# A trunk of four layers on one NeuronCore: GpSimd makes one weight tile's low half behind each running-mean mixer, and the first block's means and its add into h move forward

## The chip, the cores and the metric

The kernel runs on one core of one Trainium2 chip. The metric is the device time in microseconds, the median of several executions. Lower is better.

## What is computed

The input x has 512 tokens of 1024 channels; 16 meta tokens stand ahead of it, so the trunk works on 528 tokens. Four layers follow, each a mixer and a SwiGLU feed-forward network (FFN), and a final norm. Layers 0 and 3 have the running-mean mixer, layer 1 differential attention, layer 2 a conformer convolution. Cut to what matters here:

```python
def pool_mixer(h, w, b, scale):                 # layers 0 and 3
    for g, win in enumerate((2, 4, 8, 16)):
        hg = h[..., g * 256:(g + 1) * 256]
        groups.append(trailing_mean(hg, win) - hg)
    pooled = jnp.stack(groups, axis=2)
    mixed = jnp.einsum('blgc,gcd->blgd', pooled, w).reshape(B_, L, D_MODEL)
    return (mixed + b) * scale

for i in range(DEPTH):
    y = rmsnorm(h, norm_mix_g[i])
    h = h + mixer(y)
    h = h + (silu(n @ w_gate) * (n @ w_up)) @ w_down      # n = rmsnorm(h, norm_ffn_g[i])
```

All is float32.

## The kernel before

**Split operands.** TensorE multiplies rounded operands (fp32r). Each operand is cut into a high half, which is the value rounded (ScalarE, `ACT.Copy` into an fp32r tile), and a low half, the value less the high one (VectorE). A product is then three matmuls: high by high, low by high, high by low. For a weight tile, ScalarE's `split_hi` makes `w_hi` from `w_raw` and VectorE's `split_lo` (L2258, the instruction is L2264) makes `w_lo`. For the activations ScalarE makes `y_hi` (L1762) and VectorE `y_lo` (L2267, instruction L2270).

**Weight tiles.** The weights come as a long row of tiles of up to 128x1024 through four slots of `w_raw`, `w_hi` and `w_lo`. SyncE loads a tile into a slot when `lo_ready`, a semaphore that counts the low halves made so far, has passed the slot's last user. `hi_ready` counts the high halves. TensorE waits for `lo_ready` before it uses a tile. The mixer's own four tiles are `tile0` to `tile0 + 3`; tiles `tile0 + 4` and `tile0 + 5` are the first gate and up tiles of the FFN behind it.

**Layout.** Channels lie on partitions: `h` has 8 blocks (`blk(m.h, d)`) of 128 channels by 528 tokens. The norm's factor of a token is applied later, where tokens are on partitions or to the product, so `y_hi` and `y_lo` of block d need only h of block d and the gain column.

**The mixer** first multiplies the weights with tokens on partitions, in five tiles of tokens (`rows_times_weights`, L1004; 128, 128, 128, 127 and 32 rows). ScalarE and VectorE bring the products, scaled by the token's norm factor, from PSUM into `z_hi` (L1823) and `z_lo` (L2394, five instructions, each counted by `z_ready`). Then `windows(d)` multiplies block d of z by a band matrix, which takes the running means less the value itself (L1043, L1044, L1045 and L1052), tile after tile into two PSUM banks; with the last tile's matmul it counts `pooled`. VectorE's `add_windows(d)` (L2366) adds the block, times the scale, into h and counts `h_ready`. The bias comes into h ahead of that: by ScalarE in layer 0, by GpSimd (L933, eight adds) in layer 3.

**Behind the mixer** stands the head of the FFN (`head_by_blocks`, L1082). TensorE's stream there: six unread rows (matmuls whose result nobody reads, L1090), the means of blocks 0 and 1 without their last tile of 32 tokens, the last tile of both, eight unread rows, the means of block 2, four unread rows, the wait for `lo_ready` of the two FFN tiles, and then, block by block, the FFN's first products (`chunk`, L946) with the means of block k + 3 behind block k. In the means of block 0, `z_of` waits for four z tiles before the first and for the fifth before the last; block 1 has no such wait. `windows(d)` for d of 2 and more waits for h of block d - 2, whose banks it takes over.

VectorE's queue in the same place: the five `z_lo`, `split_lo` of tile 4, `add_windows(0)`, `split_lo` of tile 5, `y_lo` of block 0, then `add_windows(1)`, and further on alternately. ScalarE's: the five `z_hi`, `split_hi` of tiles 4 and 5, then `y_hi` and the square of each block (L1833). GpSimd adds up the squares (`sum_squares`, L799: a memset of `sumsq` at L808, then a loop of eight adds at L819, each behind a semaphore), which TensorE sums over channels at the end of the head (L960).

All orders are written out by hand; each engine runs its own queue in order, and the engines meet at semaphores.

Of the kernel before, what the change touches and what calls it, by code (L numbers as in the profile page):

```python
# [27 lines left out]
F32 = mybir.dt.float32  # L28
F32R = mybir.dt.float32r
I32 = mybir.dt.int32  # L30
ALU = mybir.AluOpType
# [27 lines left out]
TILES = 5  # L59
# [13 lines left out]
SLOTS = 4  # L73
# [481 lines left out]
def trunk(nc, a, out):  # L555
    cols, first = plan()
    tiles = len(cols)
    ctx = ExitStack()
    with ctx:
        m = Memory(nc, ctx)  # L560
# [201 lines left out]
        def _(pool):  # L762
# [36 lines left out]
            def sum_squares(r, hn):  # L799


                wait(pool, s.token_sums, r)
                wait(pool, s.rstd_sums, spreads(r))
                if r not in SUMS_OF_SQUARES:
                    pool.wait_ge(s.h_ready, NB * hn + 1)
                elif r in (R_FFN1, R_POOL3):
                    pool.wait_ge(s.square_ready, squares_before(r) + 1)
                pool.memset(m.sumsq[:, :], 0.0)  # L808
                pool.drain()
                with pool.Fori(0, NB) as d:  # L810
                    if r in SUMS_OF_SQUARES:
                        pool.wait_ge(s.square_ready, d + (squares_before(r) + 1))
                        square = blk({R_FFN1: m.o_square, R_FFN2: m.cv_square}.get(r, m.x_square), d)
                    else:
                        pool.wait_ge(s.h_ready, d + (NB * hn + 1))
                        pool.tensor_tensor(m.square[:, :], blk(m.h, d), blk(m.h, d), ALU.mult)
                        pool.drain()
                        square = m.square[:, :]
                    pool.tensor_tensor(m.sumsq[:, :], m.sumsq[:, :], square, ALU.add).then_inc(s.sumsq_ready, 1)  # L819
                    pool.drain()  # L820


            pool.wait_ge(s.table_in, 16)
            pool.memset(m.rel[:, REL_N:], 0.0)
            for i0, n, b in bucket_runs():
                last = pool.tensor_copy(m.rel[:, i0:i0 + n], m.table[:, b:b + 1].to_broadcast([HEADS, n]))
            pool.drain().then_inc(s.rel_ready, 1)
            sum_squares(R_FFN0, H_POOL0)
            sum_squares(R_ATTN, H_FFN0)

# [100 lines left out]
            for d in range(NB):  # L931
                pool.wait_ge(s.y_ready, NB * Y_POOL3 + d + 1)
                pool.tensor_tensor(blk(m.h, d), blk(m.h, d), m.pool_bs[:, 1, d:d + 1].to_broadcast([P, TOK]), ALU.add)\  # L933
                    .then_inc(s.h_biased, 1)

            sum_squares(R_FFN3, H_POOL3)


        @block.tensor
        def _(pe):  # L940
# [134 lines left out]
            def pair_layer(name, n, e0, r, yn, hn, t0, half, conv=False, pooled=None):  # L1075
# [6 lines left out]
                def head_by_blocks():  # L1082

                    if pooled is None:
                        pe.wait_ge(s.h_ready, NB * hn + 4)
                    else:
                        def unread_rows(n):

                            for _ in range(n):
                                pe.matmul(ps[:, 2, 0:HALF], m.z_hi[:, 0, 0:P], m.z_hi[:, 0, 0:HALF], start=True, stop=True)  # L1090

                        pe.wait_ge(s.z_ready, TILES * pooled + 2)
                        unread_rows(6)
                        for d in range(2):
                            windows(d, pooled, hn, range(TILES - 1))
                        for d in range(2):
                            windows(d, pooled, hn, (TILES - 1,))
                        unread_rows(8)
                        windows(2, pooled, hn)
                        unread_rows(4)  # L1100
                    pe.wait_ge(s.lo_ready, tile0 + 2)
                    for k in range(NB):
                        pe.wait_ge(s.y_ready, NB * yn + k + 1)
                        for c in range(2):
                            if r == R_FFN1 and k == 0 and c == 1:
                                pe.wait_ge(s.h_ready, NB * hn + 7)
                            mm = chunk(2 * c, half, (tile0 + c) % SLOTS, k * P, operand(m.y_hi, k, t0, half),
                                       operand(m.y_lo, k, t0, half), k == 0, k == NB - 1)
                            if k == NB - 1:
                                mm.then_inc(s.tile_used, 1)  # L1110
                        if pooled is not None and k + 3 < NB:
                            windows(k + 3, pooled, hn)
                    sum_tokens(r)
# [1143 lines left out]
        def _(dve):  # L2257
# [99 lines left out]
            def pool_layer(name, which, r, yn, hn, row):  # L2357
# [32 lines left out]
                for i in range(TILES):  # L2390
                    base, n = 2 * (i % 4), TILE_ROWS[i]
                    dve.wait_ge(s.z_hi_ready, TILES * which + i + 1)
                    two = [t[0:n, i, :].rearrange("p (b n) -> p b n", b=2) for t in (m.z_lo, m.z_hi)]
                    dve.scalar_tensor_tensor(out=two[0], in0=ps[0:n, base:base + 2, :], scalar=m.tok_r[0:n, i:i + 1],  # L2394
                                             in1=two[1].bitcast(F32), op0=ALU.mult, op1=ALU.subtract)\
                       .then_inc(s.z_ready, 1)
                split_lo(tile0 + 4, 0, 0, cols[tile0 + 4])
                add_windows(0)
                split_lo(tile0 + 5, 0, 0, cols[tile0 + 5])
                y_lo(0, yn, row, 0, TOK)  # L2400
                for d in range(1, NB):
                    add_windows(d)
# [684 lines left out]
```

## Time and profile before

| | |
|---|---|
| median of 3 executions | 2008.43 us (2007.77 to 2008.64) |
| profiled execution, its own time | 2008.29 us |
| its span, first to last instruction | 2006.5 us |
| mean granted TensorE clock | 0.999 |
| TensorE matmul busy | 1989.3 us (99%) |
| TensorE weight load busy | 1934.6 us (96%) |
| VectorE busy | 1570.3 us (78%) |
| ScalarE busy | 915.4 us (46%) |
| GpSimd busy | 203.1 us (10%) |

The span is the time between the first and the last instruction of one execution; the execution's own time is 1.79 us longer. The first mixer's means begin at about 33 us of the span, the second's at about 1633 us. In the rows below the engines are PE (TensorE matmul), PEld (its weight loads), DVE (VectorE), ACT (ScalarE), POOL (GpSimd); an instruction reads `out<-in partitions x elements`, and a bracket at a row's end is the idle time before it and what released it.

### The profile page before, as it was taken

The numbers are of one execution on the slowest core, as the hardware profiler recorded it, in microseconds if no ns is written. First come the engines' busy times: TensorE is split into PE (matmuls) and PEld (weight loads), VectorE is DVE, ScalarE is ACT, GpSimd is POOL, SyncE is SP. The second block draws the span as 40 slices with busy tenths as digits, with TensorE's granted clock in tenths as the row PEclk, the third lists the DMA queues.
The fourth block names the chain that finished last, engine by engine and source line by source line (L and its number), as shares of the span: only waits on it lengthen the run. The fifth ranks groups of instructions, "written<-read, shape, count | busy, mean of one in ns | idle before, by whom it ended". The sixth has DMA issues, their size and how long they took to land.

```text
span 2006.5 us, 40536 instructions
## 1 busy us (share of the span) xinstructions
PE 1989.3 (99%) x16016; PEld 1934.6 (96%) x16016; DVE 1570.3 (78%) x2221; ACT 915.4 (46%) x1472; POOL 203.1 (10%) x317
## 2 busy tenths in 40 slices
PE   9999999999999999999999999999999999999998
PEld 8999999999998999999999999999999998999997
DVE  6797778767877788877869886697788768977794
ACT  7443334346666443433458755343343354433342
POOL 5000000331111200000051102000000140000000
PEclk9999999999999999999999999999999999999999
DMA  5423243332211224333336531233342423333332
GB/s 169 139 85 105 84 125 85 90 123 64 62 51 58 85 85 127 93 87 92 111 101 148 126 90 56 87 97 89 105 125 67 125 75 97 106 92 100 89 106 95
DMA packets 304529, 195.24 MB, mean 97 GB/s; under 512 B 7354, under 2 KB 297147, under 8 KB 304148
## 3 DMA queue, kind: packets, MB, share of 16 engines
q1 hardware_dynamic: 298972, 175.08, 30.5%
q0 software_dynamic: 4240, 14.09, 3.3%
q10 hardware_dynamic: 1192, 4.34, 0.6%
q8 instruction: 86, 1.41, 0.3%
q14 instruction: 39, 0.32, 0.1%
HBM read 179.45 MB, written 6.44 MB: 93 GB/s over the span
## 4 chain that ended last, share of the span: by engine, by line
PE 87%; DVE 6%; issue 2%; ACT 2%; DVEq 2%; DMA 1%; POOLq 0%; SPq 0%; POOL 0%; ACTq 0%
PE ps L946 43%; PE ps L1230 32%; PE ps L1069 2%; PE ps L1341 2%; PE ps L1004 1%; PE ps L1052 1%; PE ps L1413 1%; DVE w_lo L2264 1%; DVE w_lo L2503 1%; PE ps L1454 1%; DVEq L2539 1%; DVEq L2508 1%; DVE y_lo L2503 0%; DMA w_raw<-in_ffn_w_down 0%; DMA x_rows<-in_x 0%
## 5 line engine op out<-in xcount | busy, mean ns | idle before, releaser
L1230 PE MATMUL ps<-t_lo,y_hi 128*128 128x264 f32 (+1 forms) x1008 | 285.7, 283 | 0.0
L1230 PE MATMUL ps<-t_lo,w_hi 128*128 128x264 f32 (+1 forms) x1008 | 285.7, 283 | 0.0
L1230 PE MATMUL ps<-t_hi,w_lo 128*128 128x264 f32 (+1 forms) x1008 | 285.4, 283 | 0.0
L1230 PE MATMUL ps<-t_hi,y_lo 128*128 128x264 f32 (+1 forms) x1008 | 285.3, 283 | 0.0
L1230 PE MATMUL ps<-t_hi,w_hi 128*128 128x264 f32 (+1 forms) x1008 | 285.1, 283 | 0.1
L1230 PE MATMUL ps<-t_hi,y_hi 128*128 128x264 f32 (+1 forms) x1008 | 284.8, 283 | 0.0
L1881 ACT ACTIVATE w_hi<-w_raw 128x1024 fp32r<-128x1024 f32 (+1 forms) x108 | 127.8, 1201 | 329.4 <-PE ps L946 193.2
L946 PE MATMUL ps<-hid_hi,w_hi 128*128 128x264 f32 (+1 forms) x1184 | 265.4, 296 | 0.6 <-DVE hid_lo L2559 0.5
L946 PE MATMUL ps<-hid_lo,w_hi 128*128 128x264 f32 (+1 forms) x1184 | 264.6, 296 | 0.0
L946 PE MATMUL ps<-hid_hi,w_lo 128*128 128x264 f32 (+1 forms) x1184 | 264.2, 296 | 0.0
L946 PE MATMUL ps<-y_hi,w_hi 128*128 128x264 f32 (+1 forms) x1088 | 241.1, 298 | 1.8 <-POOLq L914 0.8
L946 PE MATMUL ps<-y_lo,w_hi 128*128 128x264 f32 (+1 forms) x1088 | 233.5, 291 | 0.0
L946 PE MATMUL ps<-y_hi,w_lo 128*128 128x264 f32 (+1 forms) x1088 | 233.4, 291 | 0.0
L1881 ACT ACTIVATE y_hi<-w_raw 128x1024 fp32r<-128x1024 f32 (+1 forms) x108 | 125.8, 1197 | 166.6 <-DVE w_raw L2513 133.9
L946 PEld LDWEIGHTS ps<-hid_hi,w_hi 128*128 128x128 f32 x1184 | 187.2, 188 | 7.2 <-DVE hid_lo L2559 1.6
L946 PEld LDWEIGHTS ps<-hid_lo,w_hi 128*128 128x128 f32 x1184 | 187.6, 188 | 5.5
L946 PEld LDWEIGHTS ps<-hid_hi,w_lo 128*128 128x128 f32 x1184 | 187.4, 188 | 5.6
L1230 PEld LDWEIGHTS ps<-t_hi,w_hi 128*128 128x128 f32 x1008 | 189.8, 188 | 0.6 <-DVE h L2599 0.5
L1230 PEld LDWEIGHTS ps<-t_hi,y_hi 128*128 128x128 f32 x1008 | 189.8, 188 | 0.0
L1230 PEld LDWEIGHTS ps<-t_lo,w_hi 128*128 128x128 f32 x1008 | 189.5, 188 | 0.1
L1230 PEld LDWEIGHTS ps<-t_hi,w_lo 128*128 128x128 f32 x1008 | 189.5, 188 | 0.0
L1230 PEld LDWEIGHTS ps<-t_hi,y_lo 128*128 128x128 f32 x1008 | 189.5, 188 | 0.0
(362 smaller groups left out, 4364.3 us busy)
## 6 DMA issues: line engine op xcount, KB each, us to landing
w_raw<-in_ffn_w_gate SPq DMA_DIRECT2D x88, 512.0 KB, 5.1
w_raw<-in_ffn_w_up SPq DMA_DIRECT2D x88, 512.0 KB, 4.8
w_raw<-in_ffn_w_down SPq DMA_DIRECT2D x70, 512.0 KB, 4.3
w_raw<-in_ffn_w_down SPq DMA_DIRECT2D x24, 384.0 KB, 4.3
w_raw<-in_attn_w_qkv SPq DMA_DIRECT2D x16, 512.0 KB, 3.8
w_raw<-in_conv_w_in SPq DMA_DIRECT2D x16, 512.0 KB, 4.1
w_lo<-w_raw POOLq DMA_DIRECT2D x16, 512.0 KB, 5.0
w_raw<-in_attn_w_qkv SPq DMA_DIRECT2D x16, 256.0 KB, 2.9
```

The costliest lines, as they stand in the source:

```text
L946: mm = pe.matmul(ps[:, bank + hf, 0:half], w[:, slot, col:col + P], x(hf), start=begin and w is m.w_hi and n == 0, stop=end and w is m.w_lo)
L1004: mm = pe.matmul(out, y[:, at:at + rows], w[:, (t0 + g) % SLOTS, k * 256:(k + 1) * 256], start=k == 0 and n == 0, stop=k == 1 and n == 2)
L1052: mm = pe.matmul(out[:, c0:c1], z, m.bands[0:TILE_ROWS[i], g, at:at + c1 - c0], start=i == 2 and n == 0, stop=i in (1, 4) and n == 1)
L1069: mm = pe.matmul(ps[:, 4 * par + 2 + r, 0:cols_n], w[rows, par, :, :].rearrange("p t c -> p (t c)")[:, pairs_of_taps], u[rows, par, (j - r ...
L1230: mm = pe.matmul(ps[:, bank, 0:hw], w[:, at:at + P], b[:, t, k, 0:hw], start=k == 0 and n == 0, stop=k == 3 and n == 2)
L1341: mm = pe.matmul(bank, x, w, start=False, stop=k == LAST_F - 1 and n == 2)
L1413: mm = pe.matmul(ps[:, (4, proj_banks(par, 1))[part] + c, col:col + k1 - k0], q[rows, 0, q0:q0 + P], k[rows, 1, k0:k1], start=n == 0, stop ...
L1454: mm = pe.matmul(ps[:, 4, i * P:QT * P], v, w, start=False, stop=i == QT - 1 and x == 2)
L1881: act.activation(hi[:, sub * SUB:(sub + n_sub) * SUB], src, ACT.Copy).then_inc(s.op_hi, 1)
L2264: dve.tensor_tensor(m.w_lo[:, slot, 0:n], m.w_raw[:, slot, 0:n], m.w_hi[:, slot, 0:n].bitcast(F32), ALU.subtract).then_inc(s.lo_ready, 1)
L2503: dve.tensor_tensor(lo[:, at], raw_of(kind, c0, c1), hi[:, at].bitcast(F32), ALU.subtract)\
L2508: dve.drain()
```

## The change

Three engines' orders change, behind both mixers.

- TensorE: block 0's last tile of means stands ahead of block 1, and block 1 is done whole behind it. The unread rows ahead of block 2 are six instead of eight.
- VectorE: `add_windows(0)` comes first behind the five `z_lo`, then `split_lo` of tile 4. `split_lo` of tile 5 is gone, so that `y_lo` of block 0 follows directly.
- GpSimd: a new function, `second_tile`, waits for tile 5's high half, makes its low half, drains, waits until `lo_ready` has counted all tiles before it, drains again and counts `lo_ready`. It is called ahead of the sum of squares for the FFN's norm; in layer 3 that is behind the eight bias adds.

```diff
--- before.py
+++ after.py
@@ -820,11 +820,21 @@
                     pool.drain()
 
 
+            def second_tile(t):
+
+                pool.wait_ge(s.hi_ready, t + 1)
+                pool.tensor_tensor(m.w_lo[:, t % SLOTS, :], m.w_raw[:, t % SLOTS, :], m.w_hi[:, t % SLOTS, :].bitcast(F32),
+                                   ALU.subtract)
+                pool.drain()
+                pool.wait_ge(s.lo_ready, t)
+                pool.drain().then_inc(s.lo_ready, 1)
+
             pool.wait_ge(s.table_in, 16)
             pool.memset(m.rel[:, REL_N:], 0.0)
             for i0, n, b in bucket_runs():
                 last = pool.tensor_copy(m.rel[:, i0:i0 + n], m.table[:, b:b + 1].to_broadcast([HEADS, n]))
             pool.drain().then_inc(s.rel_ready, 1)
+            second_tile(first["pool0"] + 5)
             sum_squares(R_FFN0, H_POOL0)
             sum_squares(R_ATTN, H_FFN0)
 
@@ -933,6 +943,7 @@
                 pool.tensor_tensor(blk(m.h, d), blk(m.h, d), m.pool_bs[:, 1, d:d + 1].to_broadcast([P, TOK]), ALU.add)\
                     .then_inc(s.h_biased, 1)
 
+            second_tile(first["pool3"] + 5)
             sum_squares(R_FFN3, H_POOL3)
 
 
@@ -1091,11 +1102,10 @@
 
                         pe.wait_ge(s.z_ready, TILES * pooled + 2)
                         unread_rows(6)
-                        for d in range(2):
-                            windows(d, pooled, hn, range(TILES - 1))
-                        for d in range(2):
-                            windows(d, pooled, hn, (TILES - 1,))
-                        unread_rows(8)
+                        windows(0, pooled, hn, range(TILES - 1))
+                        windows(0, pooled, hn, (TILES - 1,))
+                        windows(1, pooled, hn)
+                        unread_rows(6)
                         windows(2, pooled, hn)
                         unread_rows(4)
                     pe.wait_ge(s.lo_ready, tile0 + 2)
@@ -2394,9 +2404,8 @@
                     dve.scalar_tensor_tensor(out=two[0], in0=ps[0:n, base:base + 2, :], scalar=m.tok_r[0:n, i:i + 1],
                                              in1=two[1].bitcast(F32), op0=ALU.mult, op1=ALU.subtract)\
                        .then_inc(s.z_ready, 1)
+                add_windows(0)
                 split_lo(tile0 + 4, 0, 0, cols[tile0 + 4])
-                add_windows(0)
-                split_lo(tile0 + 5, 0, 0, cols[tile0 + 5])
                 y_lo(0, yn, row, 0, TOK)
                 for d in range(1, NB):
                     add_windows(d)
```

TensorE in the first mixer, from the third tile of block 0's means (the pair 128x272) on; `bands` is the band matrix, and the new lines L1054, L1055, L1056 and L1063 are L1043, L1044, L1045 and L1052 of before. Before:

```order
L1052 MATMUL ps<-bands,z_hi 128x272
L1052 MATMUL ps<-bands,z_lo 128x272
L1052 MATMUL ps<-bands,z_hi 128x144
L1052 MATMUL ps<-bands,z_lo 128x144
L1043 MATMUL ps<-bands,z_hi 128x256
L1044 MATMUL ps<-bands,z_lo 128x256
L1045 MATMUL ps<-bands,z_hi 128x16
L1052 MATMUL ps<-bands,z_hi 128x128
```

And now:

```order
L1063 MATMUL ps<-bands,z_hi 128x272
L1063 MATMUL ps<-bands,z_lo 128x272
L1063 MATMUL ps<-bands,z_hi 128x144
L1063 MATMUL ps<-bands,z_lo 128x144
L1063 MATMUL ps<-bands,z_hi 128x32
L1063 MATMUL ps<-bands,z_lo 128x32
L1054 MATMUL ps<-bands,z_hi 128x256
L1055 MATMUL ps<-bands,z_lo 128x256
```

The pair 128x32, the last tile, stands behind block 0's other tiles, where block 1 used to begin.

VectorE in the first mixer, from the fourth `z_lo` on (L2376 is the add into h, L2366 before; L2274 and L2280 are L2264 and L2270). Before:

```order
L2394 SCALAR_TENSOR_TENSOR z_lo<-ps,tok_r,z_hi 127x1024
L2394 SCALAR_TENSOR_TENSOR z_lo<-ps,tok_r,z_hi 32x1024
L2264 TENSOR_TENSOR w_lo<-w_raw,w_hi 128x1024
L2366 SCALAR_TENSOR_TENSOR h<-ps,vec,h 128x528
L2264 TENSOR_TENSOR w_lo<-w_raw,w_hi 128x1024
L2270 SCALAR_TENSOR_TENSOR y_lo<-h,vec,y_hi 128x528
L2366 SCALAR_TENSOR_TENSOR h<-ps,vec,h 128x528 x2
```

And now:

```order
L2404 SCALAR_TENSOR_TENSOR z_lo<-ps,tok_r,z_hi 127x1024
L2404 SCALAR_TENSOR_TENSOR z_lo<-ps,tok_r,z_hi 32x1024
L2376 SCALAR_TENSOR_TENSOR h<-ps,vec,h 128x528
L2274 TENSOR_TENSOR w_lo<-w_raw,w_hi 128x1024
L2280 SCALAR_TENSOR_TENSOR y_lo<-h,vec,y_hi 128x528
L2376 SCALAR_TENSOR_TENSOR h<-ps,vec,h 128x528 x2
```

One `w_lo` is gone, and the add of the first block stands ahead of the other.

GpSimd behind its constant tables (`rel`), before the FFN's sum of squares. Before:

```order
L826 COPY rel<-table 8x27
L826 COPY rel<-table 8x37
L808 MEMSET sumsq 128x528
L810 UNCONDITIONAL_BRANCH
L810 ISA
```

And now:

```order
L835 COPY rel<-table 8x27
L835 COPY rel<-table 8x37
L826 TENSOR_TENSOR w_lo<-w_raw,w_hi 128x1024
L808 MEMSET sumsq 128x528
L810 UNCONDITIONAL_BRANCH
L810 ISA
```

The subtraction of 128x1024 stands between the tables and the memset of `sumsq`.

## Rows read from the trace of the kernel before

**Rows 1.** The page: busy us, share, instructions; the chain that ended last, by engine.

```profile
PE 1989.3 (99%) x16016; PEld 1934.6 (96%) x16016; DVE 1570.3 (78%) x2221; ACT 915.4 (46%) x1472; POOL 203.1 (10%) x317
...
PE 87%; DVE 6%; issue 2%; ACT 2%; DVEq 2%; DMA 1%; POOLq 0%; SPq 0%; POOL 0%; ACTq 0%
```

**Rows 2.** Chain of waits, first mixer: start us, us, what.

```profile
32.31 0.73 PE ps L1090 x6
...
39.03 1.44 PE ps L946 x12
```

**Rows 3.** Timeline, weight loads, first mixer: start us, us, engine, line, what.

```profile
32.98 0.19 PEld L1043 LDWEIGHTS ps<-bands,z_hi 128*128 128x128 f32 x1 [0.16 <-DVE z_lo L2394]
...
34.02 0.19 PEld L1043 LDWEIGHTS ps<-bands,z_hi 128*128 128x128 f32 x1
...
35.77 1.02 PEld L1090 LDWEIGHTS ps<-z_hi 128*128 128x128 f32 x8
36.72 0.19 PEld L1043 LDWEIGHTS ps<-bands,z_hi 128*128 128x128 f32 x1
...
38.06 0.18 PEld L1052 LDWEIGHTS ps<-bands,z_lo 32*128 32x128 f32 x1
38.27 0.54 PEld L1090 LDWEIGHTS ps<-z_hi 128*128 128x128 f32 x4
38.75 0.30 PEld L946 LDWEIGHTS ps<-y_hi,w_hi 128*128 128x128 f32 x2
```

**Rows 4.** Timeline, weight loads, second mixer.

```profile
1636.63 0.19 PEld L1043 LDWEIGHTS ps<-bands,z_hi 128*128 128x128 f32 x1
...
1638.64 0.19 PEld L946 LDWEIGHTS ps<-y_hi,w_hi 128*128 128x128 f32 x1
```

**Rows 5.** Timeline, VectorE, first mixer.

```profile
33.49 1.27 DVE L2394 SCALAR_TENSOR_TENSOR z_lo<-ps,tok_r,z_hi 32x1024 fp32r<-32x1024 f32 x1 [0.56 <-ACT z_hi L1823]
...
36.50 1.20 DVE L2264 TENSOR_TENSOR w_lo<-w_raw,w_hi 128x1024 fp32r<-128x1024 f32 x1
37.63 0.75 DVE L2270 SCALAR_TENSOR_TENSOR y_lo<-h,vec,y_hi 128x528 fp32r<-128x528 f32 x1
38.31 1.42 DVE L2366 SCALAR_TENSOR_TENSOR h<-ps,vec,h 128x528 f32<-128x528 f32 x2
```

**Rows 6.** Timeline, VectorE, second mixer.

```profile
1633.49 1.27 DVE L2394 SCALAR_TENSOR_TENSOR z_lo<-ps,tok_r,z_hi 32x1024 fp32r<-32x1024 f32 x1 [1.35 <-ACT z_hi L1823]
...
1635.83 0.75 DVE L2366 SCALAR_TENSOR_TENSOR h<-ps,vec,h 128x528 f32<-128x528 f32 x1
```

**Rows 7.** Timeline, ScalarE, first mixer.

```profile
33.36 1.99 ACT L1757 ACTIVATE w_hi<-w_raw 128x1024 fp32r<-128x1024 f32 x2
...
37.25 0.63 ACT L1833 ACTIVATE x_square<-h 128x528 f32<-128x528 f32 x1
```

**Rows 8.** Timeline, GpSimd, first mixer.

```profile
38.07 1.51 POOL L819 TENSOR_TENSOR sumsq<-sumsq,x_square 128x528 f32<-128x528 f32 x1 [11.14 <-ACT x_square L1833]
...
42.42 1.33 POOL L819 TENSOR_TENSOR sumsq<-sumsq,x_square 128x528 f32<-128x528 f32 x1 [0.55 <-ACT x_square L1833]
```

**Rows 9.** GpSimd by line and form: busy us, mean ns, idle before.

```profile
L933 POOL TENSOR_TENSOR h<-h,pool_bs 128x528 f32<-128x528 f32 x8 | 8.2, 1065 | 5.2 <-DVEq L2317 5.2
...
L861 POOL TENSOR_TENSOR o_t<-o_t,o_x 128x5 f32<-128x5 f32 x14 | 2.8, 196 | 2.0 <-issue 0.3
```

**Rows 10.** Timeline, GpSimd, conv output.

```profile
1230.40 1.78 POOL L819 TENSOR_TENSOR sumsq<-sumsq,cv_square 128x528 f32<-128x528 f32 x1 [25.02 <-ACT cv_square L2238]
1233.15 1.32 POOL L819 TENSOR_TENSOR sumsq<-sumsq,cv_square 128x528 f32<-128x528 f32 x1 [0.97 <-ACT cv_square L2238]
```

**Rows 11.** Timeline, VectorE, conv output.

```profile
1231.58 1.68 DVE L2264 TENSOR_TENSOR w_lo<-w_raw,w_hi 128x1024 fp32r<-128x1024 f32 x1
1233.18 1.86 DVE L2270 SCALAR_TENSOR_TENSOR y_lo<-h,vec,y_hi 128x528 fp32r<-128x528 f32 x1
```

**Rows 12.** Timeline, weight loads, second mixer, seventh block.

```profile
1654.87 0.19 PEld L946 LDWEIGHTS ps<-y_hi,w_hi 128*128 128x128 f32 x1 [0.46 <-DVE y_lo L2270]
```

## Prediction

> **What bounds the kernel now.** Start with the page's busy table. TensorE is busy 99% of the span and VectorE 78%, and the chain that ended last is 87% TensorE [rows 1]. An edit here is worth what it does to TensorE's stream; work taken off VectorE earns nothing by itself.
>
> Next, the chain of waits around the first mixer. From the six unread rows at 32.31 us to the first product of the FFN (L946) at 39.03 us it is TensorE alone [rows 2]: two blocks' means, eight unread rows, the third block's means, four unread rows. The reader is to see that no other engine is in it. Means and unread rows just cover what VectorE and ScalarE need to make the first operand. The weight loads give the same stretch finer, and I time TensorE by them: the first FFN load is at 38.75 us in the first mixer [rows 3] and at 1638.64 in the second [rows 4]. VectorE's timeline shows the margin: w_lo of the second tile ends at 36.50 + 1.20 = 37.70 us, the first y_lo at 37.63 + 0.75 = 38.38, 0.37 us before that load [rows 5]. In the second mixer the engines that feed it stand at the same offsets from 1600 us. There the third block's means waited for h of block 0: its add ended at 1635.83 + 0.75 = 1636.58 [rows 6] and the load came at 1636.63 [rows 4]. So a wait's end shows in a load 0.05 us later.
>
> **TensorE: the order of the means.** Block 0's last tile of means now stands ahead of block 1's. It needs the fifth z_lo, which ends at 33.49 + 1.27 = 34.76 us, and at 1634.76 in the second mixer [rows 5, 6]. In the first mixer block 1 began at 34.02 [rows 3], with nothing to wait for; now TensorE stands until 34.76 + 0.05 = 34.81. From there: the last tile's two loads and the step to the next block, 0.12 + 0.21 us (the row at 38.06 is the second load of such a pair, the next thing follows at 38.27), so block 1 begins at 35.14. A whole block takes 36.72 to 38.27 = 1.55 us: the unread rows begin at 36.69 instead of 35.77. Eight of them took 35.77 to 36.72 = 0.95 us, six take 0.72: the third block's means begin at 37.41 instead of 36.72, and the first FFN load could come at 39.44 instead of 38.75, **+0.69 us**. In the second mixer the same end of z_lo puts those means at 1637.41 against 1636.63 [rows 4], **+0.78 us**. This is all loss: two unread rows less give back 0.24 us, the new wait takes more. It stays even if all that follows is wrong.
>
> **VectorE and GpSimd: who makes what.** VectorE loses one w_lo and adds block 0 into h first. Block 0's means now end about 35.2 us, so the add (0.75 us) runs from 35.3 to 36.0, half a microsecond earlier than now. Alone that would bring y_lo to 37.9. But GpSimd's subtraction comes between. ScalarE's second w_hi ends at 33.36 + 1.99 = 35.35 us [rows 7]. GpSimd answers ScalarE in 0.19 us (x_square ends at 37.25 + 0.63 = 37.88, its add starts at 38.07) [rows 7, 8], so it starts at 35.54, while VectorE still adds block 0.
>
> Its price isn't in the trace, since GpSimd makes no 128x1024 subtraction. A two-operand instruction over 5 columns takes 0.196 us, the bias add over 528 columns 1.065 us [rows 9], the square add over 528 columns 1.32 us [rows 10]. By the first and the last, 1024 columns take 0.196 + 1019 × (1.32 − 0.196)/523 = 2.39 us. With the bias add, one of whose operands is a broadcast column, it is 1.89 us; in plain proportion to the square add 2.56 us. I take 2.39, since the square add too reads two full operands, and keep both ends. GpSimd ends at 37.93 us (37.43 to 38.10).
>
> Does VectorE's own w_lo, next in its queue at 36.0, run beside it? The conv output says no [rows 10, 11]. GpSimd's add ran from 1233.15 to 1234.47; VectorE's y_lo, begun at 1233.18, took 1.86 us instead of 0.75. Before it GpSimd's 1.78 us add ended at 1232.18, and the w_lo begun at 1231.58 took 1.68 us instead of 1.20 and ended at 1233.26, 1.08 us after GpSimd. So instructions that read two SBUF operands exclude each other whole, while the h adds, which read PSUM and one SBUF operand, are not lengthened: two of them took 1.42 us from 38.31 on, beside GpSimd's add of 38.07 to 39.58 [rows 5, 8]. Hence w_lo ends at 37.93 + 1.08 = 39.01 us, y_lo of block 0 another 38.38 − 37.70 = 0.68 later, at 39.69, and the first FFN load about 0.06 after it, at 39.75: **+1.00 us**. In the second mixer, at 1639.75: **+1.11 us**. These contain the part above; they aren't added to it. GpSimd's own signal needs its end, the w_lo at 39.01 and a drain; its whole turn between two adds is idle for 0.55 us [rows 8], so I put it at 39.2 to 39.5, just in time.
>
> The Trainium skill (SBUF — State Buffer, Who interferes with whom) has this exclusion as a lock held for the whole instruction, taken by issue order, for a VectorE instruction with two SBUF inputs against a GpSimd one that reads SBUF. A section of the same page, on the intuition of a bandwidth pool, has the blocked instruction (there GpSimd behind VectorE) start about 115 ns after the other's end. By that w_lo would end at 39.25, and the sum would be 0.48 us higher; I go by the 1.08 us of the row.
>
> **GpSimd's queue.** The sum of squares stands behind the new tile. Its memset and first add move from 38.07 to about 40.4 us. An add and its turn are 1.33 + 0.55 = 1.88 us [rows 8], against a block of TensorE's of 1.44 + 1.55 = 3.0 us [rows 2, 3], so GpSimd has caught up by the fifth block, and the token sums come behind the eighth. In the second mixer the eight bias adds (8.2 us together [rows 9]) stand before the new wait and are over when the fifth z_lo is. SyncE refills the tile's slot 1.6 us later, but ScalarE takes no tile from it before the eighth block. I cost all of this at nothing.
>
> **Does the delay last?** Behind the mixers TensorE waits for VectorE or ScalarE work that it fed itself, such as the 0.46 us for y_lo [rows 12], and transfers make 1% of the chain [rows 1]. So the delay goes to the end one to one: 1.00 + 1.11 = +2.11 us on the profiled execution's 2008.29, which is **2010.4 us** (on the median of 2008.43 it would be 2010.5). A measurement of this kernel can tell about 0.2% (4.0 us) from no change, so this is "same", leaning slower.
>
> **Rivals.** *No collision* (0.12): the subtraction is at its fast end, or lives beside VectorE's. Then only TensorE's new wait is left, 0.69 + 0.78 = +1.47: 2009.8. For it: the price is estimated. Against it: [rows 10, 11].
>
> *Gain* (0.07): z_lo of the last 32 rows signals well before its record ends, so there is no new wait, and two unread rows less per mixer are the effect: 2 × −0.24, 2007.8. Against it: the load at 32.98 did wait for z_lo [rows 3].
>
> *Spill* (0.12): GpSimd's late first square add takes its turn just before y_lo of block 1, which is due at 39.75 + 1.44 + 1.55 = 42.7 and by my working ends at 42.4. Each mixer loses up to 0.4 us more: 2011.2.
>
> *Slower by over 0.2%* (0.04): GpSimd does not catch up, and a square add runs each time that VectorE comes to y_lo of block 6. TensorE waits there already (0.46 us in the second mixer) [rows 12], so y_lo longer by 1.86 − 0.75 = 1.11 us [rows 11] is paid in full. If it also meets y_lo of block 7, it is 2.2 us a mixer: 2010.4 + 4.4 = 2014.8. It decides if GpSimd's turn is over some 2.6 us and not 1.88.
>
> **How the numbers follow.** Forecast 0.65; the others 0.12, 0.07, 0.12, 0.04. The forecast's own range is 2009.7 (GpSimd at 1.89 us) to 2010.9 (the longer blocking of the page's figure). For eight in ten, with the 0.9 us by which the shown runs differ, I take 2008.6 to 2012.0; it leaves out the gain and the slower case. Faster by over 0.2% would take 4 us that nothing here offers: 0.01. Slower by over 0.2%: 0.04. Same: 0.95.
>
> **What would show it.** TensorE's loads: a gap of about 0.65 us before 34.81 in the first mixer and 0.85 in the second, released by z_lo; a second one of 0.3 us ahead of the first FFN load, released by y_lo. GpSimd: the subtraction at 35.5, 2.4 us long. VectorE: w_lo recorded from 36.0 with 3.0 us instead of 1.2. It is wrong if w_lo keeps 1.2 us beside GpSimd, if the FFN load follows the unread rows without a gap, or if new gaps stand ahead of later blocks.

## The result, and the profile after

The changed kernel takes 2011.16 us (median of 22 executions, 2009.25 to 2018.66) against 2008.45 (22 executions, 2007.47 to 2010.21). The ratio is 1.0017, with a 95% interval of 1.0011 to 1.0022. It is slower by 2.7 us in the median and by 3.5 us in the mean (2012.00 against 2008.53), which is still within 0.2%. The two differ because the changed kernel's executions spread over 9.4 us instead of 2.7. Its fastest is 1.8 us over the fastest of before.

| | before | after |
|---|---|---|
| median | 2008.45 us | 2011.16 us |
| profiled execution, its own time | 2008.29 us | 2010.39 us |
| its span | 2006.5 us | 2008.7 us |
| mean granted TensorE clock | 0.999 | 0.999 |
| highest of 22 | 2010.21 us | 2018.66 us |

The page of the changed kernel: span, busy us with shares and instructions, and the chain that ended last. They answer to [rows 1].

```profile
span 2008.7 us, 40532 instructions
...
PE 1989.7 (99%) x16012; PEld 1934.2 (96%) x16012; DVE 1570.9 (78%) x2219; ACT 915.3 (46%) x1472; POOL 209.3 (10%) x319
...
PE 81%; DVE 8%; DVEq 4%; issue 3%; ACT 2%; DMA 1%; POOLq 0%; SPq 0%; POOL 0%; ACTq 0%
```

Busy time says little here: TensorE's is 0.4 us longer, and the rest of the 2.2 us of span is idle time of TensorE's. The chain has more VectorE in it; I rest nothing on that.

TensorE's weight loads in the first mixer (start us, us, engine, line, what, idle before and its releaser). Line L1063 is L1052 of before, L1101 is L1090 and L957 is L946. They answer to [rows 3].

```profile
34.24 0.19 PEld L1063 LDWEIGHTS ps<-bands,z_lo 127*128 127x128 f32 x1
35.12 0.18 PEld L1063 LDWEIGHTS ps<-bands,z_hi 32*128 32x128 f32 x1 [0.70 <-DVE z_lo L2404]
...
35.45 0.19 PEld L1054 LDWEIGHTS ps<-bands,z_hi 128*128 128x128 f32 x1
...
36.96 0.79 PEld L1101 LDWEIGHTS ps<-z_hi 128*128 128x128 f32 x6
37.68 0.19 PEld L1054 LDWEIGHTS ps<-bands,z_hi 128*128 128x128 f32 x1
...
39.22 0.53 PEld L1101 LDWEIGHTS ps<-z_hi 128*128 128x128 f32 x4
40.00 0.30 PEld L957 LDWEIGHTS ps<-y_hi,w_hi 128*128 128x128 f32 x2 [0.25 <-issue]
```

And in the second mixer; they answer to [rows 4].

```profile
1635.83 0.18 PEld L1063 LDWEIGHTS ps<-bands,z_hi 32*128 32x128 f32 x1 [0.92 <-DVE z_lo L2404]
...
1638.39 0.19 PEld L1054 LDWEIGHTS ps<-bands,z_hi 128*128 128x128 f32 x1
...
1640.70 0.19 PEld L957 LDWEIGHTS ps<-y_hi,w_hi 128*128 128x128 f32 x1 [0.24 <-issue]
```

Each mixer shows both idles that the prediction named: 0.70 and 0.92 us ahead of block 0's last tile, released by z_lo, and about 0.25 us ahead of the first FFN load. The input's transfer took a little longer in this execution, so everything begins 0.3 us later; I count from the start of the fifth z_lo, at 33.80 us here. The first FFN load stands 40.00 − 33.80 = 6.20 us behind it. Before it was 38.75 − 33.49 = 5.26 us [rows 3, 5]. That is +0.94 us. In the second mixer z_lo begins at 1634.51, so the load is 6.19 behind it against 5.15 before [rows 4, 6], +1.04 us.

VectorE (L2376 is the add into h, L2274 w_lo, L2280 y_lo) and then GpSimd, first mixer. They answer to [rows 5] and [rows 8].

```profile
33.80 1.27 DVE L2404 SCALAR_TENSOR_TENSOR z_lo<-ps,tok_r,z_hi 32x1024 fp32r<-32x1024 f32 x1 [0.54 <-ACT z_hi L1833]
35.63 0.77 DVE L2376 SCALAR_TENSOR_TENSOR h<-ps,vec,h 128x528 f32<-128x528 f32 x1 [0.56 <-PE ps L1063]
36.31 2.89 DVE L2274 TENSOR_TENSOR w_lo<-w_raw,w_hi 128x1024 fp32r<-128x1024 f32 x1
39.13 0.76 DVE L2280 SCALAR_TENSOR_TENSOR y_lo<-h,vec,y_hi 128x528 fp32r<-128x528 f32 x1
```

```profile
35.74 2.38 POOL L826 TENSOR_TENSOR w_lo<-w_raw,w_hi 128x1024 fp32r<-128x1024 f32 x1 [9.18 <-ACT w_hi L1767]
39.39 0.54 POOL L808 MEMSET sumsq<- 128x528 f32 x1 [1.26 <-POOLq L830]
40.33 1.33 POOL L819 TENSOR_TENSOR sumsq<-sumsq,x_square 128x528 f32<-128x528 f32 x1 [0.41 <-issue]
```

Here is the loss. GpSimd's subtraction runs from 35.74 to 38.12 us, 2.38 us. VectorE is through with the add of block 0 at 36.40 and has w_lo next, recorded with 2.89 us instead of 1.20. It ends at 39.20, which is 1.08 us after GpSimd. That leaves y_lo at 39.89, and the first FFN load 0.11 us later. The second mixer has the same three durations.

### The profile page after: what moved, and what is told of

Same layout as the page of the kernel before. It is cut to its first block, busy times and chain, and to the rows that moved or that the text cites. A ratio compares the mean times of both kernels' runs of the same rounds, so it can differ in the third digit from the quotient of the medians.

```text
span 2008.7 us, 40532 instructions
## 1 busy us (share of the span) xinstructions
PE 1989.7 (99%) x16012; PEld 1934.2 (96%) x16012; DVE 1570.9 (78%) x2219; ACT 915.3 (46%) x1472; POOL 209.3 (10%) x319
## 4 chain that ended last, share of the span: by engine, by line
PE 81%; DVE 8%; DVEq 4%; issue 3%; ACT 2%; DMA 1%; POOLq 0%; SPq 0%; POOL 0%; ACTq 0%
PE ps L957 40%; PE ps L1240 32%; DVEq L3009 2%; PE ps L1351 2%; PE ps L1015 1%; DVE cv L3010 1%; PE ps L1063 1%; PE ps L1423 1%; DVE w_lo L2274 1%; DVE w_lo L2512 1%; PE ps L1464 1%; DVEq L2548 1%; DVEq L2517 1%; DMA w_raw<-in_ffn_w_down 0%; DVE y_lo L2512 0%
## 5 line engine op out<-in xcount | busy, mean ns | idle before, releaser
L957 PE MATMUL ps<-hid_hi,w_hi 128*128 128x264 f32 (+1 forms) x1184 | 265.4, 296 | 0.6 <-DVE hid_lo L2568 0.6
L957 PE MATMUL ps<-hid_lo,w_hi 128*128 128x264 f32 (+1 forms) x1184 | 264.6, 296 | 0.0
L957 PE MATMUL ps<-hid_hi,w_lo 128*128 128x264 f32 (+1 forms) x1184 | 264.2, 296 | 0.0
L957 PE MATMUL ps<-y_hi,w_hi 128*128 128x264 f32 (+1 forms) x1088 | 241.2, 298 | 2.1 <-DVE cv L2983 1.1
L957 PE MATMUL ps<-y_lo,w_hi 128*128 128x264 f32 (+1 forms) x1088 | 233.5, 291 | 0.0
L957 PE MATMUL ps<-y_hi,w_lo 128*128 128x264 f32 (+1 forms) x1088 | 233.3, 291 | 0.0
L957 PEld LDWEIGHTS ps<-hid_hi,w_hi 128*128 128x128 f32 x1184 | 187.1, 188 | 7.0 <-DVE hid_lo L2568 1.3
L957 PEld LDWEIGHTS ps<-hid_lo,w_hi 128*128 128x128 f32 x1184 | 187.6, 188 | 5.5
L957 PEld LDWEIGHTS ps<-hid_hi,w_lo 128*128 128x128 f32 x1184 | 187.4, 188 | 5.7
```

What stands on the lines that cost most here:

```text
L957: mm = pe.matmul(ps[:, bank + hf, 0:half], w[:, slot, col:col + P], x(hf), start=begin and w is m.w_hi and n == 0, stop=end and w is m.w_lo)
```

## The experiments

Each timing shares its chip with the kernel before. Two theories. **Theory 1** is the prediction's: both mixers lose about a microsecond each to queues, above all to VectorE standing behind GpSimd's subtraction. **Theory 2** came with the result: TensorE's new idles let its clock fall in some executions, and that is the spread. Among the 22 timed executions, 7 have a mean granted clock of 0.997 or less, and they are the seven longest, 2012.59 us and up; 4 more are at 0.998.

### TensorE's order back

```diff
-                        windows(0, pooled, hn, range(TILES - 1))
-                        windows(0, pooled, hn, (TILES - 1,))
-                        windows(1, pooled, hn)
-                        unread_rows(6)
+                        for d in range(2):
+                            windows(d, pooled, hn, range(TILES - 1))
+                        for d in range(2):
+                            windows(d, pooled, hn, (TILES - 1,))
+                        unread_rows(8)
```

> The changed kernel with TensorE's order and its eight unread rows as before; GpSimd's tile and VectorE's order stay. Theory 1 (GpSimd's subtraction sets the first FFN load, 0.93 us later in the first mixer): no wait ahead of block 0's last tile, one gap of about 0.9 us ahead of the first FFN load in each mixer, 2.0 us over before. Rival (TensorE's new order is what costs): within 0.5 us of before. Theory 2 (a TensorE idle of 0.7 to 0.9 us lets the clock fall in some executions, which is the spread of the changed kernel from 2009.3 to 2018.7): some of its executions are 3 to 8 us over its fastest, with a mean clock under 0.998, as the idle is only moved.

Measured: 2010.32 us (2009.81 to 2012.65, 11 executions) against 2008.40, ratio 1.0012 (1.0003 to 1.0021). Its first FFN loads, first and second mixer:

```profile
39.36 0.30 PEld L957 LDWEIGHTS ps<-y_hi,w_hi 128*128 128x128 f32 x2 [0.82 <-POOLq L830]
```

```profile
1640.52 0.19 PEld L957 LDWEIGHTS ps<-y_hi,w_hi 128*128 128x128 f32 x1 [1.09 <-POOLq L830]
```

No wait stands ahead of block 0's last tile, and one idle of 0.82 and 1.09 us ahead of the FFN. The load comes 6.21 us after the fifth z_lo began in both mixers (33.15 and 1634.31 us), as in the changed kernel. The rows name GpSimd's signal, but y_lo ended at 39.25 and the load follows it by 0.11 us, as there. So in the queues TensorE's new order costs nothing that the exclusion would not cost anyway; the rival that puts the price on it falls. VectorE's w_lo begins 2.99 and 2.70 us after the fifth z_lo began (2.51 and 2.50 in the changed kernel) and is recorded with 2.42 and 2.71 us, yet it ends 1.08 us after GpSimd's subtraction all the same. So GpSimd's end sets it, not its own start. Theory 2 expected more spread than came: one execution of 11, 2012.65 us, has a mean clock under 0.999 (0.998).

### VectorE makes both tiles

```diff
-            second_tile(first["pool0"] + 5)
...
-            second_tile(first["pool3"] + 5)
...
                 add_windows(0)
                 split_lo(tile0 + 4, 0, 0, cols[tile0 + 4])
+                split_lo(tile0 + 5, 0, 0, cols[tile0 + 5])
```

> TensorE's new order and six unread rows, with VectorE making both tiles behind the add of block 0 and GpSimd none. Theory 1: only the wait for z_lo is left, 0.7 and 0.9 us, first FFN load 0.69 and 0.78 us over before: 1.45 us over before, no second gap. w_lo keeps 1.2 us. Rival (GpSimd frees VectorE and so helps): slower than the changed kernel, over 2.2 us over before. Theory 2: this gap alone gives the spread, some executions 3 to 8 us over the fastest.

Measured: 2010.93 us (2010.23 to 2016.64, 11 executions) against 2008.40, ratio 1.0015 (1.0006 to 1.0024), which is 2.5 us and not 1.45. GpSimd, VectorE (L2263 is w_lo, L2269 y_lo) and then the first FFN load, first mixer:

```profile
37.01 1.94 POOL L819 TENSOR_TENSOR sumsq<-sumsq,x_square 128x528 f32<-128x528 f32 x1 [10.54 <-ACT x_square L1832]
```

```profile
35.43 2.35 DVE L2263 TENSOR_TENSOR w_lo<-w_raw,w_hi 128x1024 fp32r<-128x1024 f32 x2
37.70 1.82 DVE L2269 SCALAR_TENSOR_TENSOR y_lo<-h,vec,y_hi 128x528 fp32r<-128x528 f32 x1
```

```profile
39.64 0.30 PEld L946 LDWEIGHTS ps<-y_hi,w_hi 128*128 128x128 f32 x2 [0.77 <-issue]
```

Both w_lo keep their 1.2 us, as expected. The expectation missed what happens next. With two tiles first, y_lo of block 0 comes at 37.70, and by then the square of block 0 is ready and GpSimd's square add has begun. So y_lo takes 1.82 us instead of 0.75, and the FFN load comes 6.73 us after z_lo began (at 32.91; 6.71 in the second mixer), 0.5 us later than in the changed kernel. The same exclusion moved to another pair of instructions. Taking the tile off GpSimd isn't enough, since its sum of squares works there too. Part of what the rival named did come, over 2.2 us over before, though the median isn't above the changed kernel's: with the add of block 0 ahead of both tiles, GpSimd's help is worth those 0.5 us a mixer, and yet both kernels are slower than before. One execution of 11, 2016.64 us, has a mean clock under 0.999 (0.995), fewer than theory 2 expected.

### The tile on GpSimd, but VectorE's first

The changed kernel with TensorE's order of before, and one line of VectorE moved:

```diff
-                add_windows(0)
                 split_lo(tile0 + 4, 0, 0, cols[tile0 + 4])
+                add_windows(0)
                 y_lo(0, yn, row, 0, TOK)
```

> GpSimd still makes the second tile, but VectorE makes the first tile's low half ahead of the add of block 0 and TensorE keeps the order of before with its 12 unread rows behind the first means. Theory 1 (the loss is VectorE's w_lo standing behind GpSimd's subtraction): w_lo takes 1.2 us and is out of the way by 2.4 us after the fifth z_lo began, GpSimd's subtraction starts behind it and ends at 4.6, y_lo ends at about 5.2 instead of 6.1, the first FFN load at 5.3 instead of 6.2 in both mixers (5.26 and 5.15 before). So 0.2 to 0.3 us over before, no spread. Rival (GpSimd is simply too slow for this tile): the load waits for GpSimd's signal, at 6.0 or later, 1.5 us and more over before.

Measured: 2008.58 us (2008.17 to 2009.18, 11 executions) against 2008.34, ratio 1.0001 (0.9992 to 1.0010). VectorE (L2275 w_lo, L2377 add, L2281 y_lo) and GpSimd, first mixer, and then the first FFN load of both mixers:

```profile
34.37 1.20 DVE L2275 TENSOR_TENSOR w_lo<-w_raw,w_hi 128x1024 fp32r<-128x1024 f32 x1
35.54 0.77 DVE L2377 SCALAR_TENSOR_TENSOR h<-ps,vec,h 128x528 f32<-128x528 f32 x1
37.11 1.28 DVE L2281 SCALAR_TENSOR_TENSOR y_lo<-h,vec,y_hi 128x528 fp32r<-128x528 f32 x1 [0.81 <-ACT y_hi L1773]
```

```profile
35.11 2.72 POOL L826 TENSOR_TENSOR w_lo<-w_raw,w_hi 128x1024 fp32r<-128x1024 f32 x1 [9.22 <-ACT w_hi L1768]
```

```profile
38.56 0.31 PEld L957 LDWEIGHTS ps<-y_hi,w_hi 128*128 128x128 f32 x2
```

```profile
1638.62 0.19 PEld L957 LDWEIGHTS ps<-y_hi,w_hi 128*128 128x128 f32 x1
```

This decides for theory 1: the kernel of "TensorE's order back" differs from this one by that line of VectorE alone, and its load stands at 6.21 us. GpSimd does the same work, and it now waits for VectorE's w_lo to end (2.72 us recorded instead of 2.38), while VectorE goes on with the add from PSUM. The FFN load is 5.39 and 5.34 us after z_lo began (33.17 and 1633.28 us): +0.13 and +0.19 us over before, where the changed kernel has +0.94 and +1.04. Nothing in the expectation was off by more than 0.1 us, and no execution has a clock under 0.999. GpSimd was not too slow for the tile. It had been put ahead of a VectorE instruction that the first FFN product waited for. Nor is anything gained by the help. In the second mixer y_lo, which stands behind h of block 0 and then behind GpSimd's subtraction, ends 0.11 us before the load. In the first the load follows the unread rows without a gap, 0.17 us after y_lo; there the +0.13 us stands already ahead of the unread rows before the third block's means, and is not GpSimd's.

### The gaps filled

```diff
                         windows(0, pooled, hn, range(TILES - 1))
+                        unread_rows(5)
                         windows(0, pooled, hn, (TILES - 1,))
```

> The changed kernel with five unread rows (0.6 us) ahead of block 0's last tile, inside the wait for z_lo. Theory 1: same first FFN load to 0.05 us, same fastest time as the changed kernel. Theory 2 (the idle ahead of the last tile lets the clock fall): the spread is gone, all executions within 1.5 us and clocks of 0.998 or 0.999. If the spread has another cause (the port, the second gap, the chip), it stays.

Measured: 2011.00 us (2010.25 to 2014.11, 11 executions) against 2008.40, ratio 1.0017 (1.0008 to 1.0026). With two unread rows more ahead of the first FFN product as well:

> As the last, with two more unread rows ahead of the first FFN product, inside the second gap of 0.25 us. Theory 1: the first FFN load within 0.1 us of the changed kernel's. Theory 2: no spread. If the second gap was the cause and the first was not, the spread goes here and stays in the kernel with the first gap filled.

Measured: 2011.32 us (2010.53 to 2012.63), ratio 1.0016 (1.0007 to 1.0025).

The first FFN load is at 6.19 to 6.22 us after z_lo in both, as theory 1 has it. Of the 22 executions one has a clock under 0.999, as theory 2 has it. But the two longest of the first kernel, 2013.87 and 2014.11 us, are not within 1.5 us of the rest as expected. The first stands at a clock of 0.999, so it is something else; the second is the one at 0.998. And the fastest are 1.0 and 1.3 us slower than the changed kernel's fastest. All three profiles with the fill (one is of a later timing) show one longer wait behind the first part of the FFN; this is the later one's:

```profile
167.49 0.30 PEld L957 LDWEIGHTS ps<-hid_hi,w_hi 128*128 128x128 f32 x2 [1.29 <-DVE hid_lo L2569]
```

It is 1.16 to 1.43 us in those three, and 0.47 before, 0.53 and 0.31 in the two profiles of the changed kernel and 0.88 with both tiles on VectorE. Its 0.6 to 0.9 us over the changed kernel's 0.53 would account for most of the 1.0 and 1.3 us. It is VectorE's hid_lo, and further back the chain hangs on transfers of w_down. Why it goes with the fill is open; I did not test it. It also shows that "the delay goes to the end one to one" holds only to within some tenths.

### The changed kernel and the filled one on one chip

> The changed kernel unaltered, beside the three others on one chip. Theory 2 (its new idles let the clock fall in some executions): again some of its executions are 3 us and more over its fastest, with clocks of 0.997 and less; fastest about 1.9 us over the fastest of before. Rival (the spread belonged to the chip or the hour of the first timing): all within 2 us of its fastest, clocks 0.999.

> The changed kernel with both gaps filled, on the same chip as the changed kernel. Theory 2: no execution with a clock under 0.998, while the changed kernel has some. If both have them or neither, the gaps aren't the cause.

Measured: the changed kernel 2011.79 us (2010.09 to 2019.01) and the filled one 2011.32 (2010.73 to 2012.98), both against 2008.13; ratios 1.0017 (1.0008 to 1.0026) and 1.0016 (1.0007 to 1.0025). Clocks of 0.997 or less: 5 of 11 executions of the changed kernel, none of 11 filled, none of 33 of before. Clocks under 0.999: 8, 1 and none. With the earlier timings it is 12 of 33 against 0 of 33 with a fill at 0.997 or less, and 19 against 2 under 0.999; in the earlier timings the two did not stand side by side. So the spread goes with the changed kernel's idles. A lower clock isn't confined to that kernel: of the 33 executions of before that stood beside TensorE's order back, both tiles on VectorE and the first fills, 2 were at 0.997 and 0.998 (2011.45 and 2011.19 us). The fill takes the longest executions away (2012.98 us against 2019.01 here) and 0.8 us off the mean, but with its longer wait it leaves the median nearly where it was.

This time the profiled execution was one of the long ones (span 2017.3 us, mean clock 0.994), so one can see where. The columns are stretch, its us, then busy time and instructions of PE, PEld, DVE, ACT and POOL, the granted clock, the DMA share and GB/s:

```profile
13.00:20.00 7.00, 7.00 (x39) 6.68 (x38) 4.43 (x9) 4.82 (x8) 4.08 (x7) 0.54 0.42 116
...
40.00:46.80 6.80, 6.80 (x32) 6.63 (x31) 4.54 (x5) 4.54 (x8) 3.98 (x5) 0.51 0.56 155
46.80:50.00 3.20, 3.20 (x27) 3.09 (x26) 1.44 (x2) 0.79 (x3) 1.17 (x1) 1.00 0.00 1
...
1644.40:1651.20 6.80, 6.80 (x27) 6.05 (x27) 4.27 (x5) 2.43 (x4) 3.94 (x5) 0.52 0.55 154
1651.20:1656.00 4.80, 4.80 (x29) 4.20 (x29) 2.26 (x4) 1.29 (x3) 2.04 (x2) 1.00 0.00 0
```

The kernel before in the same place:

```profile
13.00:20.00 7.00, 6.95 (x62) 6.61 (x60) 5.81 (x11) 6.36 (x11) 3.24 (x7) 1.00 0.65 173
...
40.00:46.80 6.80, 6.80 (x55) 6.59 (x55) 4.48 (x5) 5.70 (x10) 3.96 (x3) 1.00 0.22 66
```

Granted clock 0.51 and 0.52 is the 1.2 GHz level. It lasts for 6.8 us behind each mixer's first means. In 40.0 to 46.8 us TensorE gets through 32 matmuls where before did 55 (and also 55 from 37.1 to 43.9, where it does the same part of the work). The weight loads around the first fall:

```profile
36.56 0.19 PEld L1063 LDWEIGHTS ps<-bands,z_lo 127*128 127x128 f32 x1
37.67 0.18 PEld L1063 LDWEIGHTS ps<-bands,z_hi 32*128 32x128 f32 x1 [0.92 <-DVE z_lo L2404]
...
40.47 0.33 PEld L1054 LDWEIGHTS ps<-bands,z_hi 128*128 128x128 f32 x1
```

The idle of 0.92 us ends at 37.67. The clock is still full for 2.2 us, and from 40.47 on a load takes 0.33 us instead of 0.19. This delay has no wait in front of it: TensorE is busy all through. By the starts of the same loads on both sides of a mixer, this execution loses 2.7 us more over each mixer than the first profile of the changed kernel did. A third stretch of the kind, at 13 to 20 us, lies ahead of both mixers, behind a wait of 1.75 us for the input (1.04 before and 1.17 in the first profile of the changed kernel, where no fall followed). It cost another 2.7 us, and it lies ahead of all that the change touches. Three falls of this length, 8.1 us, are nearly all of the 8.6 us between this execution and the first profile. One or two would give about 2013 and 2016 us; that the other long executions are such is an estimate, as they have no profile.

### The kernel before with idles put in

All 18 unread rows taken out (6, 8 and 4 at their three places):

> The kernel before without the 18 unread rows behind each mixer. Its waits are then idle: about 0.8 us for the fourth z_lo, 0.9 for h of block 0, 0.3 for y_lo of block 0. Theory 1: the first FFN load follows y_lo by 0.1 us, 0.26 and 0.15 us earlier than before: fastest executions 0.4 us under before's. Theory 2: more idle than in the changed kernel, so at least as many executions of 3 us and more over the fastest, with clocks of 0.997 and less. If none, idle of this size doesn't touch the clock.

Measured: 2012.46 us (2007.89 to 2015.67, 11 executions) against 2008.13, ratio 1.0019 (1.0010 to 1.0028). Its loads that waited, first mixer:

```profile
33.27 0.19 PEld L1043 LDWEIGHTS ps<-bands,z_hi 128*128 128x128 f32 x1 [1.07 <-issue]
...
36.84 0.19 PEld L1043 LDWEIGHTS ps<-bands,z_hi 128*128 128x128 f32 x1 [0.81 <-DVE h L2363]
...
38.71 0.30 PEld L946 LDWEIGHTS ps<-y_hi,w_hi 128*128 128x128 f32 x2 [0.37 <-issue]
```

The first FFN load follows the fifth z_lo by 5.06 us instead of 5.26, and by 5.01 instead of 5.15 in the second mixer, so the queues gain nearly the 0.4 us that theory 1 said. Yet the fastest execution, 2007.89, is 0.4 us over before's fastest and not under it. 9 of 11 have a clock of 0.997 or less, the other two 0.998, and the median is 4.3 us over before. A gain of 0.3 us in the queues turned into a loss more than ten times as large.

The profiled execution is one of the two at 0.998 (2008.95 us). Its longest idle in the second mixer, and the clock from 2.3 us behind that on:

```profile
1635.81 0.19 PEld L1043 LDWEIGHTS ps<-bands,z_hi 128*128 128x128 f32 x1 [1.30 <-DVE h L2363]
```

```profile
1638.10:1641.50 3.40, 3.40 (x13) 2.91 (x12) 1.59 (x3) 2.43 (x4) 1.97 (x2) 0.50 0.60 173
```

A mean clock of 0.998 can thus hold a fall of 3.4 us, while none of the nine profiles at 0.999 or 1.000 shows one. So 0.999, and not 0.997, is the mark by which to count the executions without a fall.

Only the eight rows ahead of the third block's means taken out:

> The kernel before without the eight unread rows ahead of the third block's means: one idle of 0.9 us in each mixer, waiting for h of block 0, and the first FFN load 0.09 us earlier and the same. By the queues alone 0.1 us under before. Theory 2: one idle of this length is enough, so some executions have clocks of 0.997 and less and are 2.7 us (one fall) or more over the fastest. If none has, it takes more idle than this in a mixer, as in the kernel without any unread rows.

Measured: 2012.05 us (2010.27 to 2014.06, 11 executions) against 2008.34, ratio 1.0022 (1.0013 to 1.0031). The load that waited, and the clock in the stretch behind it in either mixer (columns as above):

```profile
36.34 0.19 PEld L1043 LDWEIGHTS ps<-bands,z_hi 128*128 128x128 f32 x1 [0.88 <-DVE h L2365]
```

```profile
38.50:42.00 3.50, 3.50 (x20) 3.50 (x18) 1.72 (x3) 3.19 (x6) 2.10 (x2) 0.51 0.62 181
1639.40:1642.80 3.40, 3.40 (x12) 2.84 (x12) 1.57 (x3) 2.43 (x4) 1.96 (x2) 0.50 0.62 175
```

One idle of 0.88 us in the first mixer and 1.10 in the second, and the clock falls behind them in this profile. It stays low for about half the time it did above, so one fall costs less than the 2.7 us which I had expected. All 11 executions have clocks of 0.997 or less, and none of the 21 of before beside them is under 0.999. By its queues this kernel ought to be 0.1 us faster than before. So the unread rows keep the clock up, and without the eight in the middle the other ten don't.

### Two unread rows fewer

```diff
                         windows(2, pooled, hn)
-                        unread_rows(4)
+                        unread_rows(2)
```

> The kernel before with two unread rows instead of four ahead of the first FFN product. The first FFN load is then bound by y_lo (0.1 us after its end) and not by the unread rows: 0.24 and 0.15 us earlier, 0.4 us under before in sum, no spread, as the idle stays under 0.1 us.

Measured: 2007.51 us (2007.03 to 2008.67, 11 executions) against 2008.13, ratio 0.9997 (0.9988 to 1.0006).

```profile
38.97 0.30 PEld L1090 LDWEIGHTS ps<-z_hi 128*128 128x128 f32 x2
39.30 0.30 PEld L946 LDWEIGHTS ps<-y_hi,w_hi 128*128 128x128 f32 x2
```

The load comes 5.01 us after the fifth z_lo began in both mixers, 0.25 and 0.14 us earlier than before, without an idle and without a clock under 0.999. The median is 0.6 us lower, which the interval doesn't tell from nothing; the loads do show 0.39 us. It is the only version here with a median under before's, and the step is too small to be more than a hint.

## Why the prediction was right, and where it wasn't

**The sum.** I forecast +2.11 us, of which +1.00 in the first mixer and +1.11 in the second. The profile has +0.94 and +1.04, and its own time is 2010.39 us against my 2010.4. That the two times meet is luck: the later input added 0.3 us, a wait in the second mixer 0.14 (below), and between the mixers 0.2 us came back (+1.24 us at 167 us of the span, +1.02 at the second mixer's fifth z_lo); the execution's time outside its span was 0.1 us shorter. The median is 2.7 us over before, not 2.1; the 11 executions at a clock of 0.999 have a median of 2010.27, 1.8 over. Each term is 0.06 to 0.07 us lower because GpSimd started earlier behind ScalarE's signal than 0.19 us, less the signal from y_lo to the load, which took 0.11 us and not 0.06.

**TensorE's order.** The stall until z_lo came as worked out: the load at 35.12 is 0.05 us behind its end at 35.07, and the third block's means begin at 37.68 − 33.80 = 3.88 us against my 3.92. It was right too that this is covered by the larger delay; with the order put back the load did not move.

**GpSimd's price.** 2.39 us from the rows of 5 and 528 columns, 2.38 measured. The other two estimates, 1.89 and 2.56, miss by 0.5 and 0.2 us; that the chosen one fits to 0.01 is luck in part.

**The exclusion.** w_lo ended 1.08 us after GpSimd, as the w_lo in [rows 11] did. On the figure of the Trainium skill (SBUF — State Buffer, the section on the bandwidth-pool intuition), a start some 115 ns after the other's end, w_lo would have ended 1.3 us after it. That figure is for GpSimd behind VectorE, and here it is the other way round. But in the kernel with the tile apart GpSimd does stand behind VectorE: its 2.38 us ended 2.26 us after w_lo (37.83 against 35.57), where the 115 ns would make 2.50. The lock itself (in the Trainium skill the same page, Who interferes with whom) is as the traces have it, down to the add from PSUM that takes 0.77 us beside GpSimd's subtraction.

**GpSimd's queue.** It caught up by the fifth block, as forecast, but not quite for nothing. The spill that I feared at block 1 was 0.09 us (y_lo 0.86 instead of 0.77 us), and no load waited for it. In the second mixer VectorE's add of block 6 came late (the cause wasn't pursued), and the square add before it overlapped y_lo of block 6. VectorE, GpSimd and the load that waited:

```profile
1655.42 0.77 DVE L2376 SCALAR_TENSOR_TENSOR h<-ps,vec,h 128x528 f32<-128x528 f32 x1 [1.11 <-PE ps L1063]
1656.11 1.66 DVE L2280 SCALAR_TENSOR_TENSOR y_lo<-h,vec,y_hi 128x528 fp32r<-128x528 f32 x2
```

```profile
1655.12 1.32 POOL L819 TENSOR_TENSOR sumsq<-sumsq,x_square 128x528 f32<-128x528 f32 x1 [1.97 <-ACT x_square L1843]
```

```profile
1657.06 0.19 PEld L957 LDWEIGHTS ps<-y_hi,w_hi 128*128 128x128 f32 x1 [0.60 <-DVE y_lo L2280]
```

The load waited 0.60 us where it was 0.46 before [rows 12]: 0.14 us. That is the mechanism of my slower rival at an eighth of its price, and it stays so also in the kernel with the tile apart, whose wait is the same 0.60.

**What failed**, though the time fell where I said, is the last step of "Does the delay last?", with the rivals built on it: the prediction counted TensorE's new idle as its own length and no more. No case in it had the clock fall, and the only one over 0.2% slower was GpSimd not catching up. In fact behind idles of 0.92 and 0.93 us the clock was at 1.2 GHz for 6.8 us in the profile that caught it, at 2.7 us for each fall. In the first timing the clock is the likely reason why the mean is 3.5 us over before and the queues account for 2.1, and it pushed executions to 2018.66, far outside my range; the median rose too but stayed inside. Before had such idles covered with unread rows [rows 2]. I read those rows as slack to be trimmed and gave back 0.24 us for two of them, where I should have asked what they keep up.

## What to carry to other kernels

When two engines exclude each other, price the helper by what stands behind it in the other engine's queue, not by its own length: the same GpSimd instruction cost 1 us a mixer ahead of VectorE's w_lo and at most 0.2 behind it. Before a wait of TensorE's is opened or a filler matmul is dropped, look at the granted clock over many executions and not in one profile: the first profile here showed none of the falls. Where two kernels differ more in the mean or in the longest execution than in the fastest, look for a clock before looking for a queue.

## What the hardware showed that wasn't expected

In the mixers, idles of TensorE's of about 1 us in an otherwise dense stream were followed by 1.2 GHz, and the fall came only 2.2 to 2.6 us behind the idle's end, while TensorE was busy. It lasted 3.4 us in two profiles and 6.8 in a third.

How often it came, counted by executions with a mean clock under 0.999, and the idles of the profile (us, first and second mixer):

| idles | executions |
|---|---|
| 0.88; 1.10, ahead of the third block's means | 11 of 11 |
| 1.07, 0.81, 0.37; 0.23, 0.39, 1.30, 0.37 | 11 of 11 |
| 0.70 to 0.93, ahead of block 0's last tile, then 0.24 to 0.25 | 19 of 33 |
| 0.60; 0.92, at the same place, then 0.77; 0.75 | 1 of 11 |
| 0.82; 1.09, ahead of the first FFN product alone | 1 of 11 |
| the changed kernel with a fill | 2 of 33 |
| none (before; the executions whose clock is on record) | 2 of 87 |
| none (the tile apart; two unread rows fewer) | 0 of 22 |

So length alone doesn't decide, and place seems to matter, though not alone either: the third and fourth rows have much the same first idle. The fourth and fifth were not timed beside the third, and what it is about the place was not tested.
